# Splitting the dot products of gathered expert rows: VectorE multiplies, ScalarE sums

## The reference

```python
def peer(h, wq, subkeys, u, v):            # T = 256 tokens, 8 heads, 16 experts per head and token
    q = (ht @ wq).reshape(T, P_HEADS, 2, P_DKH)
    s = einsum('thcd,hcnd->thcn', q, subkeys)
    s1, i1 = top_k(s[:, :, 0], 16); s2, i2 = top_k(s[:, :, 1], 16)
    sc, ci = top_k(all sums s1 + s2, 16)
    e = i1[ci // 16] * 128 + i2[ci % 16]   # expert numbers
    g = softmax(sc)
    z = einsum('thkd,td->thk', u[e], ht)   # the dots of gathered rows
    a = gelu(z) * g
    return einsum('thk,thkd->td', a, v[e]) # weighted sum of gathered rows
```

## Time and profile before

| | before |
|---|---|
| median of 3 runs | 1266.02 us (1265.32 to 1266.77) |
| the profiled execution: its own time | 1264.91 us |
| its span (first to last instruction) | 1263.1 us |
| PE busy | 1141.3 us, 90% |
| DVE busy | 920.6 us, 73% |
| ACT busy | 512.0 us, 41% |
| POOL busy | 332.8 us, 26% |
| stage of the rows, first gather issued to last dot | 320.6 to 962.8 us |

### The profile page before, as it was taken

How to read it: one execution, slowest core, us unless ns; L and a number is a source line. 1 busy time by engine, 2 the same in 40 slices (tenths; PEclk the granted TensorE clock), 3 DMA queues, 4 the chain that set the end, 5 groups by cost and what they waited for, 6 DMA issues and landing times.

```text
span 1263.1 us, 14906 instructions
## 1 busy us (share of the span) xinstructions
PE 1141.3 (90%) x5180; PEld 798.9 (63%) x5180; DVE 920.6 (73%) x1849; ACT 512.0 (41%) x994; POOL 332.8 (26%) x311
## 2 busy tenths in 40 slices
PE   5999999999799998987888878777789999999998
PEld 5989999998655454443333433333335897788887
DVE  5997987886779667777677767677756696888544
ACT  3657443545423222312222222221514477677442
POOL 4000000000356544555454444444441000000000
PEclk9999999999899999999899999898999999999999
DMA  8874577687999999999999999999997622555550
GB/s 358 330 292 176 183 297 271 212 325 280 367 423 422 425 426 426 426 427 426 426 426 427 426 427 428 425 427 426 428 424 309 220 101 73 195 193 178 196 200 34
DMA packets 58271, 406.70 MB, mean 322 GB/s; under 512 B 6964, under 2 KB 7172, under 8 KB 9684
## 3 DMA queue, kind: packets, MB, share of 16 engines
q0 software_dynamic: 38752, 273.55, 51.8%
q1 hardware_dynamic: 19444, 132.19, 28.2%
HBM read 404.66 MB, written 1.06 MB: 321 GB/s over the span
## 4 chain that ended last, share of the span: by engine, by line
PE 54%; DMA 30%; DVE 10%; issue 3%; ACT 3%; POOL 1%; SPq 0%; POOLq 0%; DVEq 0%; ACTq 0%
DMA ring<-in_peer_uv,ei 12%; DMA gbuf<-in_peer_uv,ei 12%; PE bank L836 11%; PE bank L488 5%; PE bank L492 5%; PE bank L489 5%; PE bank L996 5%; DMA wq_place<-in_peer_uv,ei 4%; PE bank L768 3%; PE bank L999 2%; PE bank L1028 2%; PE bank L1027 2%; PE bank L1026 2%; PE bank L509 2%; PE bank L503 1%
## 5 line engine op out<-in xcount | busy, mean ns | idle before, releaser
L836 PE MATMUL bank<-gbuf,dg 128*128 128x512 f32 x540 | 261.5, 629 | 53.6 <-ACT dg L1334 53.5
L1531 DVE TENSOR_TENSOR half<-ring,half 128x1024 fp32r<-128x1024 f32 x175 | 212.8, 1223 | 86.0 <-ACT half L1052 84.2
L1052 ACT ACTIVATE half<-ring 128x1024 fp32r<-128x1024 f32 x175 | 183.9, 1056 | 128.2 <-PE bank L1028 47.0
L836 PEld LDWEIGHTS bank<-gbuf,dg 128*128 128x128 f32 x540 | 105.6, 200 | 196.0 <-issue 121.7
L1993 DVE CUSTOM_DVE_ANT_0 gbuf<-gbuf,h2t 128x1024 f32<-128x1024 f32 x135 | 165.3, 1225 | 81.4 <-DMA gbuf<-in_peer_uv,ei 80.2
L2346 POOL DMA_INDIRECT gbuf<-in_peer_uv,ei x135 | 159.7, 1183 | 191.3 <-PE bank L836 118.7
L836 PE MATMUL bank<-ring,dg 128*128 128x512 f32 x356 | 172.7, 623 | 28.1 <-ACT dg L1334 28.1
L1326 ACT ACTIVATE za<-za 128x4 f32<-128x4 f32 x62 | 12.7, 205 | 399.3 <-DVE za L1993 399.3
L2346 POOL DMA_INDIRECT ring<-in_peer_uv,ei x89 | 108.4, 1218 | 169.6 <-DVE ei L1966 70.7
L1993 DVE CUSTOM_DVE_ANT_0 ring<-ring,h2t 128x1024 f32<-128x1024 f32 x89 | 108.8, 1224 | 54.9 <-DMA ring<-in_peer_uv,ei 54.7
L836 PEld LDWEIGHTS bank<-ring,dg 128*128 128x128 f32 x356 | 70.1, 201 | 120.8 <-issue 81.7
(11 more groups left out here) (432 smaller groups left out, 1888.6 us busy)
## 6 DMA issues: line engine op xcount, KB each, us to landing
ring<-in_weights SPq DMA_DIRECT2D x114, 1024.0 KB, 4.9
gbuf<-in_weights SPq DMA_DIRECT2D x4, 1024.0 KB, 10.0
gbuf<-in_peer_uv,ei POOLq DMA_INDIRECT x135, 23.2
wq_place<-in_weights SPq DMA_DIRECT2D x2, 1024.0 KB, 6.5
bcs<-in_b_ada POOLq DMA_DIRECT2D x3, 512.0 KB, 12.2
ring<-in_peer_uv,ei POOLq DMA_INDIRECT x89, 23.0
xs<-in_x SPq DMA_DIRECT2D x2, 512.0 KB, 4.0
ya<-in_weights SPq DMA_DIRECT2D x1, 1024.0 KB, 17.4
```

Of the source, the lines that this page charges most:

```text
L836: r = e.matmul(acc[a][j][:, :], dg[:, i % 4, :], expert_rows(i)[:, 1024 + 512 * j:1536 + 512 * j], start=h == 0 and k == 0, stop=h == 7 an ...
L1052: e.activation(h, v, AF.Copy).then_inc(*o.inc(s_hi, split(n)))
L1531: e.tensor_tensor(l, v, h.bitcast(f32), ALU.subtract).then_inc(*o.inc(s_lov, split(n)))
```

## The change

Three things change. For the rows below 248, `dot(i)` is a plain multiply on VectorE, in place, without a sum. ScalarE gets a new function `row_sum(i)`: a Copy of the 128x1024 product onto itself with the engine's accumulator writing the sum into `za`. Four of them stand ahead of each gelu in ScalarE's list. And `weight(g)` moves in VectorE's list: it stood in iteration 4g+3, behind the pieces of routing (for g = 0 in iteration 4), and now stands in iteration 4g+4, directly behind `dot(4g+4)`. Rows 248 to 255 keep the fused dot.

```diff
+        def row_sum(i):
+            n, row = i // 16, expert_rows(i)[:, 0:1024]
+            e.wait_ge(s_dot, i + 1)
+            e.activation(row, row, AF.Copy, accum_out=za[:, n % 2, i % 16:i % 16 + 1]).then_inc(*o.inc())
+
         def gelu(g):
             n, c = g // 4, 4 * (g % 4)
-            e.wait_ge(s_dot, 4 * g + 4)
+            for i in range(4 * g, 4 * g + 4):
+                row_sum(i)
+            e.wait_ge(*o.now)
             if n >= 2 and c == 0:
                 e.wait_ge(s_dg, 16 * n - 16)
             e.activation(za[:, n % 2, 16 + c:20 + c], za[:, n % 2, c:c + 4], AF.Gelu_apprx_tanh).then_inc(
@@ dot(i)
             e.wait_ge(*landed(i))
-            e.tensor_tensor_reduce(row, row, h2t[:, ITS[n][0], :], 1.0, 0.0, ALU.mult, ALU.add,
-                                   za[:, n % 2, i % 16:i % 16 + 1]).then_inc(*o.inc(s_dot, i + 1))
+            if i < LAST:
+                e.tensor_tensor(row, row, h2t[:, ITS[n][0], :], ALU.mult).then_inc(*o.inc(s_dot, i + 1))
+            else:
+                e.tensor_tensor_reduce(row, row, h2t[:, ITS[n][0], :], 1.0, 0.0, ALU.mult, ALU.add,
+                                       za[:, n % 2, i % 16:i % 16 + 1]).then_inc(*o.inc(s_dot, i + 1))
@@ main loop of VectorE
         for i in range(256):
             dot(i)
+            if 0 < i <= LAST and i % 4 == 0:
+                weight(i // 4 - 1)
             for _ in range(ROUTE_AT[i]):
                 if next(rt, rt) is rt and n_rt < 15:
                     n_rt += 1
                     rt = route(n_rt)
             if i == 12:
                 tokens_done(1)
-            if i < LAST and i % 4 == 3 and i > 3 or i == 4:
-                weight(i // 4 if i > 4 else 0)
```

## The result

The changed kernel takes 1276.41 us (median of 4 runs, 1275.43 to 1277.33) where the kernel before takes 1265.67 us (4 runs of the same session). The ratio is 1.0083, 95% interval 1.0071 to 1.0095, so 9.0 to 12.0 us slower. The forecast was 1274.0 us, 8.0 us slower, with 0.85 for slower.

The account below looks back on a forecast made before the run. The prediction took the 256-row stage to be paced by its DMA gathers. It added 6.6 us at the start and 1.4 at the end, 8.0 on the profiled 1264.91, giving 1272.9, or 1274.0 us as median; range 1268.5 to 1279.

Parts of the forecast that it names:

- The middle is free: Mid-stage: ScalarE has room and places freed 2 to 3 us later are absorbed by 17 us of queue: 0.
- VectorE's edit: Dots below row 248: at most 20.6 us of accumulator reads go away, hidden behind the gathers' pace; booked 0.
- VectorE was the limit: Rival for the whole kernel: 20.6 us of removed VectorE work would show, down to 1245 us; chance 0.04.
- ScalarE's edit: Each row sum on ScalarE takes 1.07 us, 4.3 us more per group; only the fourth lies in the path.
- The steps of the start: First gelu to row 30: sums, slow clock and moved weights make TensorE's row 16 8.6 us late; 6.6 us lost.
- The slack of the gathers: Queued gathers: lateness costs only beyond time to landing minus 5.4 us; 2.3 us free at row 16, 2.0 at row 30.
- a landing lost there is never made up: Early stage, rows 16 and 30: lost landings stay lost, since the DMA engines have no spare time behind.
- Those two thin places: Rows 16 and 30, early in the stage: little queue, landing after 7.7 and 7.4 us, where the change can hurt.
- The end: Last rows: weight(61) behind dot 248 moves TensorE's row 244 by 2.2 us; 1.4 us on the path.
- a lighter start: Rival at the start: TensorE keeps full clock, gather floor about 1 us lower; 1271.4 us, chance 0.20.
- not slower: Rival: the queue absorbs the start, nothing lost at row 30, 1.4 us left at the end; 1267.4 us, chance 0.11.
- ScalarE late behind groups 56 and 57: Rival: squares, table loads and sums delay the gelu and hold up dots; some 3 us more, 1277 us, chance 0.17.

Follow-up runs that it names:

- sums for group 0 alone: Kernel before, with multiply and ScalarE row sums for rows 0 to 3 only; other rows fused, all weights in old places: 1270.37 us, ratio 1.0037.
- the start as before: Changed kernel, but groups 0 to 7 (rows 0 to 31) keep fused dots and old weight places: 1266.59 us, ratio 1.0012 against the kernel before.
- weight(61) alone: Kernel before, with only the weight of group 61 moved, behind dot 248: 1268.35 us, ratio 1.0024.
- all weights moved: Kernel before, dots still fused, with every weight moved one dot later and no row sums: 1271.30 us, ratio 1.0052.
- weight(4) alone: Kernel before, with only the weight of group 4 moved, behind dot 20: 1265.76 us, ratio 1.0006.
- row 30 held to row 21: Kernel before, with row 30's gather waiting until TensorE is done with row 21, a hold of 3.4 us: 1268.37 us, ratio 1.0024.
- sums alone: Kernel before, with the change's row sums on ScalarE but every weight in its old place: 1272.78 us, ratio 1.0061.
- group 0 fused: Changed kernel, with rows 0 to 3 fused as before and without row sums: 1271.15 us, ratio 1.0048 against the kernel before.
- row 30 held to row 20: Kernel before, with row 30's gather waiting until TensorE is done with row 20, a hold of 1.7 us: 1265.66 us, ratio 1.0008.
- start and end as before: Changed kernel, but groups 0 to 7 and 61 as before, so 53 of 62 groups keep the change: 1263.92 us, ratio 0.9993 against the kernel before.
- matmuls at row 0: Changed kernel, with ten extra unused 128x256 matmuls on TensorE ahead of row 0: 1274.49 us, ratio 1.0079 against the kernel before.

## Why the prediction was right in sign and stage, and short by 2.7 us

**The middle is free: confirmed.** 53 groups with four sums more on ScalarE and the weight one dot later make no difference (0.9984 to 1.0002), as the 17 us of queue said. The exception is the stretch around 930 us, where two other kernels lost time (below).

**VectorE's edit at nothing: confirmed.** The plain multiply takes 1.226 us, the fused one 1.225. The read was 0.083 us, but VectorE's busy time fell by 2.1 us in all, not 20.6. Nothing of it showed in the time (the 53 groups: -2.0 to 0.3 us), and the rival "VectorE was the limit" is out.

**ScalarE's edit: confirmed.** I took 1.07 us per sum; the step is 1.04. First gelu 4.1 us later (forecast 4.3).

**The steps of the start: confirmed, each within 0.4 us.** Row 0's records took 1.7 us more (forecast 1.6; bounds 0 and 1.6 in the text, slightly passed). Net of 1.0 us, row 4 is 7.0 late, row 8 and `route(2)` 7.2 (forecast 7.2), row 16 8.3 (forecast 8.6: group 4's weight added 1.1 us, not 1.4), row 30's gather 8.3 (forecast 8.6).

**The slack of the gathers: this is the term that was mis-sized.** The prediction priced a late gather by "only when x is over its time to landing minus 5.4", and so took 2.0 us off at row 30. The kernels with one gather held contradict it: holds of 1.7 and 3.4 us lost 1.5 and 3.5 us of DMA time where the rule gives 0 and 1.4, and the longer one cost 3.0 us (1.9 to 4.2) by the runs. By the table, a shift of row 30 comes out whole at the last dot, within the scatter, in kernels from 2.3 to 6.5 us. The 5.4 us itself was right for the gather that arrives late (5.5 to 6.5 from issue to landing). What it leaves out is the rate of the rows behind it: 339 to 364 GB/s at a DMA share of 0.93 to 0.97, for ten us behind the held gather.

In the changed kernel itself the last dot is 7.2 us late (forecast 6.6) and row 30's gather 8.3, but the 1.1 us between them are not slack that was left at row 30. Counted by packets, the gathers' queue is 9.0 us late, net, when its bytes reach 40 rows, still 8.9 at 240 rows, and 7.1 at its end. So the whole delay, and a little more, passed row 30, and 1.8 us came back in the last rows. There most DMA engines have run out of work while VectorE still waits for landings. Windows just ahead of the last dot, before and after:
```profile
955.00:960.00 5.00, 5.00 (x13) 2.25 (x12) 2.99 (x7) 1.21 (x4) 0.00 (x0) 1.00 0.11 46
```
```profile
965.00:970.00 5.00, 5.00 (x13) 2.19 (x12) 3.01 (x7) 1.21 (x4) 0.00 (x0) 1.00 0.44 147
```
The last packets of the last row came 7.1 us behind those of the row ahead of it before, and 5.5 us in the changed kernel. Why this tail is shorter there was not tested. The prediction's "a landing lost there is never made up" does not hold for these 1.8 us.

**A thin place was missed.** "Those two thin places" were rows 16 and 30. There is an earlier one: row 10, which waits for TensorE's row 0. Its landing took 8.2 us before, so by the prediction's own rule it had 2.8 us, and it came 5.8 us late in the changed kernel. The first stop of the DMA engines is there, and the kernel with sums for group 0 alone shows that the loss is made there and that row 30 adds nothing to it. In the changed kernel 8.6 of the 9.9 us of DMA time lost in 330 to 430 us are lost by 385 us, before row 30; 2.2 of them fall in 370 to 375 us, during the long issue of row 17, which no step of the prediction has (0.7 in these five us in the kernel with sums for group 0 alone, whose issues are all under 2.0 us). By the prediction's own rule these early rows would have lost 3.0 us (row 10) and 3.7 (row 16), less than its 6.6 for row 30. The total came near the forecast because, as it said of rows 16 and 30, these are the same microseconds, and partly by luck: the 2.0 us that were taken off as slack and were not there, and the 1.8 us that came back in the last rows and were not foreseen, nearly cancel.

**The end.** Forecast 1.4 us. With TensorE at full clock it is just that: 1.4 us in the kernel with the start as before, where row 244 took 1.98 us. With the clock down at row 244 it is 2.2 us in the changed kernel and 3.1 in the one with weight(61) alone. The prediction had booked the slow restart at row 0 but not here, where the pause is ahead of the most exposed twelve rows. The four pauses of 4.65 to 4.94 us ahead of rows 0 and 244 all ended in a slow row. Pauses of 2.23 to 2.50 us did so at row 16 with all weights moved and at row 244 of the changed kernel, and did not at row 16 of the changed kernel and with weight(4) alone. At row 244 a pause of 2.60 us kept the clock before and lost it in the kernel with row 30 held to row 21. So the length of the pause alone does not tell, and the end can differ by a slow restart where the edit gives no reason for it.

**What is left.** 7.2 + 2.2 = 9.3 us is inside the 9.0 to 12.0 of the ratio; 8.0 was 1.0 below its lower end. The rest of the profile's 11.2 us lies ahead of the stage and behind L864, where nothing differs, and is scatter. The rivals: "a lighter start" and "not slower" are out, since TensorE lost its clock at row 0 and its shift at row 30 was 8.3 us. Of "ScalarE late behind groups 56 and 57", the changed kernel shows VectorE waiting 2.31 us for one gelu at 925.77 and no DMA time lost; the kernels with sums alone and with group 0 fused did lose 3.7 and 2.6 us around there. What sets them apart is TensorE's row 232, for whose place row 244's gather waits: a pause of 5.39 and 3.53 us and a restart at the lower clock there, 1.83 us and no restart in the changed kernel. That fits, and was not tested. Why few queued gathers run below the full rate is open as well. The packets show the form of it: in 750 to 760 us before, each packet of 8 KB took 309 ns, all 523 of them; in 395 to 405 us of the kernel with row 30 held to row 20 the 437 packets took 351 ns on average, and single ones up to 1148. That weight(0), weight(1) and the first four sums would cost less if another list order freed row 10's place earlier was not tried; no version beat the kernel before beyond the measurement.

## What to carry to other kernels

In a stage that is paced by DMA, find every place where the queue of transfers is thin, the first refill above all, by listing issue and landing in order of time; do not stop at the smallest landing time. There, book a late transfer at its whole lateness: the time to landing minus that of a lone transfer is not slack, because rate is lost before the queue is empty. Delays of several transfers in a row overlap, so the largest counts and not the sum. Work added to an idle engine was free here in the deep part of the queue and cost its full latency at the two ends; moving it there (or leaving the ends as they were, as with start and end as before) decides the result.

## What was not expected of the hardware

- The DMA engines' busy share can be 0.96 to 0.98 at 347 to 364 GB/s, when 426 is the full rate. The share alone hides a loss of a sixth.
- A pause of 2.29 us on TensorE ended once at the lower clock (granted 0.67 from 387.58 to 392.80 us, rows 16 and 17: 1.7 us more) and once at the upper (1.00), in two kernels with the same pause at the same row.
- A gather's issue on GpSimd is held until VectorE's dot ends. In the kernel before, 99 of the 256 issues began 0.1 to 1.0 us into a dot, and all 99 ended 0.79 to 0.84 us behind the end of that dot; issues with no dot near took 0.94 us in the median. One pair of the 99:
```profile
419.83 1.23 DVE L1993 CUSTOM_DVE_ANT_0 gbuf<-gbuf,h2t 128x1024 f32<-128x1024 f32 x1 [1.19 <-DMA gbuf<-in_peer_uv,ei]
420.15 1.72 POOL L2346 DMA_INDIRECT ring<-in_peer_uv,ei  x1 [0.70 <-PE bank L836]
```
  The plain multiply does the same: 79 of 79 in the changed kernel, where all dots but the last eight are plain.
- The gather of row 17 in the changed kernel took GpSimd 4.56 us to issue, and the DMA rate in 370 to 375 us was 242 GB/s. Of the 256 issues of before none took over 2.0 us. While it was issued, VectorE ran three plain multiplies without a gap:
```profile
369.00 3.49 DVE L2001 TENSOR_TENSOR gbuf<-gbuf,h2t 128x1024 f32<-128x1024 f32 x3
```
  The issue ended at 373.31 us, 0.82 us behind the last of the three. The kernel with sums alone and the one with matmuls at row 0 have the same pair: three multiplies in 3.49 and 3.65 us, and one gather issued in 3.43 and 3.42 us, which ended 0.81 us behind the third and the second of them. The kernel before has only two fused dots back to back there, and its issues end with a single dot. Whether the plain multiply is the reason was not tested. For it: in the kernel with sums for group 0 alone three fused dots stand back to back at the same place, and the issue among them took 1.98 us. Against it: in the kernel with sums alone four other issues began in a plain multiply with the next one directly behind it, and each ended 0.81 us behind the first. Each kernel shows one such long issue at most, and the mean of the 256 issues is 1.15 us in the changed kernel against 1.21 before. If it is the multiply, it is a cost that the prediction did not book.

The Trainium skill (SBUF — State Buffer, SBUF: two separate sides) says that VectorE and GpSimd share a pair of ports, and that a VectorE operation with two inputs in SBUF keeps it for its whole instruction from a GpSimd operation that reads SBUF. Both kinds of dot have two inputs in SBUF, and the gather takes its indices from there; the 99 and 79 issues that end with a dot agree with it.
